# First attention of a two-layer model: the softmax weights are turned undivided and held stationary, the result is divided token by token and turned back

## The reference, cut to what matters

```
logits = einsum('..qhe,..khe->..hqk', q, k) * Dh ** -0.5 + bias      # masked: causal
p = softmax(logits)                                                    # over the keys
out = einsum('..hqk,..khe->..qhe', p, v)
mix = concatenate([y_a, y_b, y_c]); x = x + mix @ w_out
```

## Time and profile before

| | us |
|---|---|
| median of 3 runs | 1622.53 (1620.39 to 1623.35) |
| profiled execution, its own time | 1622.39 |
| its span, first to last instruction | 1620.6 |
| first attention, 221.85 to 293.08 | 71.23 |

### The profile page before, as it was taken

The page is one execution under the profiler, slowest core; times in us unless marked ns, Lnnn a source line. Parts: engine busy times, 40 slices in busy tenths (PEclk is TensorE's granted clock), DMA queues, the critical chain, the costliest instruction groups (busy, mean ns, idle before and its releaser), DMA issues.

```text
span 1620.6 us, 21424 instructions
## 1 busy us (share of the span) xinstructions
PE 1518.1 (94%) x6882; PEld 1184.9 (73%) x6882; DVE 924.2 (57%) x1300; ACT 575.8 (36%) x917; POOL 724.9 (45%) x366
## 2 busy tenths in 40 slices
PE   6989967999999999999988989999899999999997
PEld 4755634777888888888766778666787888888886
DVE  5299977468264554785568351666446655664121
ACT  3322256233231322342476332655223323232222
POOL 1589844434544444434323434535243444444442
PEclk7999979999999999989999999999999999999998
DMA  5588920135455554533323324311132333332332
GB/s 188 145 187 196 224 65 27 52 116 166 151 161 164 162 164 154 169 98 89 82 73 84 81 65 106 53 34 40 52 91 65 104 92 103 91 104 86 96 94 88
DMA packets 285060, 176.72 MB, mean 109 GB/s; under 512 B 43794, under 2 KB 269458, under 8 KB 282954
## 3 DMA queue, kind: packets, MB, share of 16 engines
q1 hardware_dynamic: 285002, 175.98, 39.1%
HBM read 173.29 MB, written 5.80 MB: 111 GB/s over the span
## 4 chain that ended last, share of the span: by engine, by line
PE 40%; issue 36%; POOL 13%; DVE 4%; DMA 3%; ACT 2%; SPq 1%; POOLq 0%; DVEq 0%; ACTq 0%
POOL WL L638 11%; PE ps L1823 11%; PE ps L1825 11%; PE ps L1824 11%; DMA vb<-bv_dram 2%; PE ps L2204 2%; POOL kvp L666 1%; PE ps L2044 1%; PE ps L2018 1%; PE ps L2215 1%; PE ps L2228 1%; DVE qs L1356 1%; DVE scanned L1348 1%; ACT LP L888 1%; DVE LP L1410 1%
## 5 line engine op out<-in xcount | busy, mean ns | idle before, releaser
L638 POOL TENSOR_TENSOR WL<-Wraw,WH 128x1024 fp32r<-128x1024 f32 (+2 forms) x239 | 572.6, 2397 | 797.9 <-ACT WH L760 797.9
L1823 PE MATMUL ps<-actH,WH 128*128 128x512 f32 x1256 | 502.9, 400 | 36.0 <-POOL WL L638 17.1
L760 ACT ACTIVATE WH<-Wraw 128x1024 fp32r<-128x1024 f32 (+2 forms) x239 | 246.1, 1031 | 728.7 <-PE ps L1825 635.5
L1825 PE MATMUL ps<-actH,WL 128*128 128x512 f32 x1256 | 491.6, 391 | 0.0
L1824 PE MATMUL ps<-actL,WH 128*128 128x512 f32 x1256 | 491.4, 391 | 0.0
L1823 PEld LDWEIGHTS ps<-actH,WH 128*128 128x128 f32 x1256 | 237.2, 189 | 116.8 <-issue 25.1
L1825 PEld LDWEIGHTS ps<-actH,WL 128*128 128x128 f32 x1256 | 237.2, 189 | 51.1
L1824 PEld LDWEIGHTS ps<-actL,WH 128*128 128x128 f32 x1256 | 237.6, 189 | 48.5 <-issue 1.9
L1823 PE MATMUL ps<-UH,WH 128*128 128x512 f32 x576 | 228.4, 397 | 10.2 <-DVE T L1677 4.1
L1825 PE MATMUL ps<-UH,WL 128*128 128x512 f32 x576 | 225.7, 392 | 0.0
L1824 PE MATMUL ps<-UL,WH 128*128 128x512 f32 x576 | 225.5, 391 | 0.0
(11 more groups left out here) (236 smaller groups left out, 1531.3 us busy)
## 6 DMA issues: line engine op xcount, KB each, us to landing
Wraw<-in_w_ff SPq DMA_DIRECT2D x64, 512.0 KB, 4.0
Wraw<-in_w_in SPq DMA_DIRECT2D x56, 512.0 KB, 4.0
wada<-in_w_ada SPq DMA_DIRECT2D x64, 384.0 KB, 4.1
Wraw<-in_w_up SPq DMA_DIRECT2D x44, 512.0 KB, 3.8
vb<-bv_dram SPq DMA_DIRECT2D x64, 256.0 KB, 4.5
Wraw<-in_w_down SPq DMA_DIRECT2D x16, 448.0 KB, 3.8
Wraw<-in_w_proj_rnn SPq DMA_DIRECT2D x16, 320.0 KB, 3.1
Wraw<-in_w_proj_mla SPq DMA_DIRECT2D x8, 512.0 KB, 3.9
```

Source lines behind the costliest of these rows:

```text
L638: nc.gpsimd.tensor_tensor(WL[slot][:, 0:kts, :], Wraw[slot][:, 0:kts, :], WH[slot][:, 0:kts, :].bitcast(F32), ALU.subtract).then_inc(s_lo, 1)
L760: A(WH[slot][:, 0:kts, :], Wraw[slot][:, 0:kts, :], ACT.Copy).then_inc(s_hi, 1)
L1823: MM(o, wh, ah, start=first, stop=False)
L1825: return MM(o, wl, ah, start=False, stop=last)
```

## The change

Nobody divides the weights in `LP` any more: `a_normalize` is gone and `a_recips` is one reciprocal a pair (128x8). `a_turn` waits for the exponentials only. `a_weigh` swaps the operands: a turned 128x128 tile of `PT` is stationary, 64 columns of `Vt` move, so bank 7 holds one query a partition and the features of both heads of each block side by side: 20 matmuls in place of 8. The new `a_scaled` on VectorE multiplies bank 7 by the reciprocals, each over 64 columns, into `a_tokens` (the first half of `oSq`, free since the gated attention). The new `a_back` on TensorE turns its four tiles back into bank 7. `pair_high` waits for that. In step p, `a_scaled(p-2)` stands on VectorE where `pair_low(p-2)` stood, `a_back(p-2)` behind the scores of block 3 on TensorE, and `pair_high(p-2)` and `pair_low(p-2)` move to the end of the step: `pair_high` in front of ScalarE's last turned copy, `pair_low` behind VectorE's.

```diff
@@ scalar
-                act.wait_ge(S(pre + "_weighted"), p + 1)
+                act.wait_ge(S("a_turned_back" if pre == "a" else "m_weighted"), p + 1)
@@
-                    if p >= 2 and i == 1:
-                        pair_high("a", p - 2, actH)
                     if 1 <= i and 1 <= p:
                         a_turned(p - 1, i - 1)
+                if p >= 2:
+                    pair_high("a", p - 2, actH)
                 if p >= 1:
                     a_turned(p - 1, TB - 1)
@@ vector
+            def a_recips(p):
+
+                dve.wait_ge(S("a_exp"), 2 * TB * (p + 1))
+                V.reciprocal(astat[:, 2, p % 2, :, :], astat[:, 1, p % 2, :, :]).then_inc(S("a_recip"), 1)
+
+            def a_scaled(p):
+
+                dve.wait_ge(S("a_recip"), p + 1)
+                dve.wait_ge(S("a_weighted"), p + 1)
+                by_head = lambda t: t.rearrange("p (g d) -> p g d", d=HEAD_DIM)
+                V.tensor_tensor(by_head(a_tokens), by_head(ps[:, 7, :]),
+                                astat[:, 2, p % 2, :, :].rearrange("p i e -> p (i e)").unsqueeze(2)
+                                .to_broadcast([P, 2 * TB, HEAD_DIM]), ALU.mult).then_inc(S("a_scaled"), 1)
@@
+                if p >= 2:
+                    pair_low("a", p - 2, actL, actH)
@@ tensor
-                    pe.wait_ge(S(f"a_normed{e}"), TB * p + i + 1)
+                    pe.wait_ge(S("a_exp"), 2 * TB * p + 2 * i + e + 1)
@@
-                for k in range(TB):
+                for i in range(TB):
                     for e in range(2):
-                        q = slice(HEAD_DIM * e, HEAD_DIM * (e + 1))
-                        mm = MM(ps[q, 7, k * P:SEQ], Vt[:, p, k, q], PT[:, e, k, k * P:SEQ], start=(k == 0), stop=(k == TB - 1))
+                        for k in range(i + 1):
+                            mm = MM(ps[:, 7, i * P + e * HEAD_DIM:i * P + (e + 1) * HEAD_DIM], PT[:, e, k, i * P:(i + 1) * P],
+                                    Vt[:, p, k, e * HEAD_DIM:(e + 1) * HEAD_DIM], start=(k == 0), stop=(k == i))
                 mm.then_inc(S("a_weighted"), 1)
+
+            def a_back(p):
+
+                pe.wait_ge(S("a_scaled"), p + 1)
+                for t in range(TB):
+                    mm = nc.tensor.transpose(ps[:, 7, t * P:(t + 1) * P], a_tokens[:, t * P:(t + 1) * P], ident)
+                mm.then_inc(S("a_turned_back"), 1)
...
```

More of the change, by code:

```diff
@@ L345, in hybrid_stack @@
         s_ev = S("block_evacuated")
+        a_tokens = oSq[:, 0:2, :].rearrange("p t c -> p (t c)")
         def wcols(name, rows0, kts):
@@ L677, in _ @@
             lows(gOut, 2, 1)
[L679 to L688, removed]
             pool.wait_ge(S("a_low"), PAIRS)
@@ L1437, in a_step @@
                         a_logits(p, i, 1)
+                    if p >= 1 and i == 0:
+                        a_recips(p - 1)
                     if p >= 2 and i == 2:
[L1439 to L1446, removed]
+                        a_scaled(p - 2)
+                    if p >= 1 and i >= 1:
+                        a_turned(p - 1, i - 1)
                 if p >= 1:
                     a_turned(p - 1, TB - 1)
+                if p >= 2:
+                    pair_low("a", p - 2, actL, actH)
             for p in range(PAIRS + 1):
                 a_step(p)
+            a_scaled(PAIRS - 1)
             pair_low("a", PAIRS - 1, actL, actH)
@@ L2053, in a_step @@
                         a_weigh(p - 2)
+                    if i == 3 and p >= 2:
+                        a_back(p - 2)
                     if i >= 1 and p >= 1:
@@ L2062, in _ @@
             a_weigh(PAIRS - 1)
+            a_back(PAIRS - 1)
             pair_product(gOut, gOut.n0, x_in, lambda k: (S("a_low"), k + 1) if k < PAIRS else (S("gla_low"), k + 1 - PAIRS),
```

## The result

The changed kernel takes 1650.85 us (median of 4 runs, 1647.64 to 1652.13) against 1622.94 (1620.39 to 1626.63): 1.0173 times as long, 95% interval 1.0157 to 1.0188. The forecast was 1634, range 1629 to 1641. The direction was right, the size 2.4 times too small. The profiled execution took 1649.94 us, its span is 1648.2.

What follows compares the result with a forecast made beforehand. The first attention was taken as a loop of waits through TensorE, VectorE and ScalarE, no engine full. Periods +5.8, two end terms +3.2 each and start -0.5 gave +11.7: 1634.1 us, range 1629 to 1641.

Steps and rivals of the forecast that it cites:

- the clock: First attention: no fall in the sum, since TensorE's new gaps are each shorter than the old 1.84 us.
- The loop: First attention, one period: weighing 4.05, turn 0.37, scores of block 2 to next weighing 7.63, together 12.05 us.
- the pace of the weighing: New weighing on TensorE: 40 load-and-multiply pairs at 0.101 us, load-bound, 4.05 us, 1.75 more than before.
- the low part: VectorE, end of each step: the next weighing waits for it, making the loop's tail 7.63 us, not 7.53.
- the turning back: TensorE, behind the scores of block 3: four transposes, 0.56 us, hidden by ScalarE's exponentials except at the end.
- The four periods: First to fifth weighing: 48.2 us at 12.05 each against 42.40 before, +5.8 us.
- the two end terms: Fifth to sixth weighing and last weighing to projection: +3.2 us each.
- the start: Before the first weighing: waits for VectorE between pair 0 and pair 1 go, -0.5 us.
- Rival 1: Weighing goes by its columns, 2.3 us, no loss: 1625.2 us, or 1622 if the clock also rises sooner; chance 7%.
- The prediction's own sign of being wrong: First attention: a granted clock of 0.50 inside the periods, listed among the signs that would show the forecast wrong.
- Rival 2: The clock falls in the new weighings: 8.0 us each, 4 us more per hit, 1638 to 1642 us; chance 12%.
- rivals 3 and 4: New weighing: loads at the transposes' pace, 0.14, 1643.4 us, chance 8%; loads not overlapped, 1647.6 us, chance 3%.

Runs made afterwards that it cites:

- e2: The changed kernel with 128 moving columns instead of 64 in each product of the weighing, waits unchanged, first head's result overwritten: 1637.14 us, ratio 1.0077.
- e6b: The changed kernel with throwaway products only right before each weighing (three, six before the last two): 1634.97 us, ratio 1.008.
- e1: The changed kernel with throwaway products both before the last turn of each pair and before each weighing: 1635.45 us, ratio 1.0067.
- e4: The kernel before, without divisions, with the new form of weighing but no scaling or turning back: 1639.61 us, ratio 1.0078.
- e8: The kernel before with undivided weights and old weighing, dividing its result per feature through eight small products in TensorE's gap: 1617.3 us, ratio 0.9965.

## Why the prediction was wrong

The step that failed is the clock: the sum had no term for its fall, and the fall cost 11.75 us before the projection and 1.2 behind it.

- **The loop: the mechanism right, the close sum luck.** Loads set the pace of the weighing, the low part is the new last wait, the scaling takes 0.60, and the turning back is hidden except at the end: as predicted. But a load and its product take 0.112 us (4.49 / 40), not the 0.101 I took: +0.44 us a weighing. The four periods are 7.6 us longer and not 5.8, the two end terms 3.4 and 3.7 and not 3.2 each. That is 2.5 us more than forecast, and the start gave 2.2 more back, so the parts sum to +12.0 against +11.7 because two errors cancel.
- **A slip in the sum.** The 42.40 us of the four periods before contain their own fall of the clock (4 x 10.20 would be 40.8). The forecast set periods without one against them and so took 1.6 us for a fall that would not come. Rival 1 used 10.20 instead; on the forecast's footing it is 1623.6 and not 1625.2.
- **The start: mis-sized.** -2.7 us instead of -0.5. With the divisions gone TensorE was busy for 4.00 us from 230 to 234 us, before for 2.71, and the clock rose about four microseconds sooner; the prediction names this only inside rival 1. The size is partly chance: counted from the first score product, the first weighing starts after 17.68 us here, 17.29 in e2 and 18.8 in e6b (less its filler), with the same code up to there, and after 20.29 in the kernel before. The rows from 230 to 238 us, before and after:

```profile
230.00:234.00 4.00, 2.71 (x10) 1.30 (x10) 3.42 (x17) 2.62 (x9) 3.11 (x3) 0.50 0.39 133
234.00:238.00 4.00, 4.00 (x13) 1.42 (x10) 2.42 (x10) 2.50 (x10) 1.86 (x3) 0.50 0.00 0
```

```profile
230.00:234.00 4.00, 4.00 (x15) 1.61 (x13) 2.13 (x9) 2.85 (x12) 0.00 (x0) 0.50 0.45 133
234.00:238.00 4.00, 2.44 (x16) 1.47 (x16) 2.30 (x8) 3.30 (x11) 0.00 (x0) 0.99 0.14 23
```

- **The clock: the step that failed.** The prediction's own sign of being wrong, a granted clock of 0.50 inside the periods, is there. Rival 2 had the right price, 4 us for a weighing at the half level (the fifth took 8.56 us where 8.0 was forecast), but 12%, and its 1638 to 1642 holds one or two hits; there were three. The argument was that "TensorE's gaps in the new period ... are each shorter than the 1.84 us" of the old one. They measured 0.1 before the turning back, 1.21 before the last turn (0.5 forecast) and 0.62 before the weighing. So the premise held in every period, and the clock fell all the same: with a pause of 0.62 us before the second weighing, and 1.47 before the fifth and sixth. The argument looked at the idle time only. The new weighing has 64 columns moving under a load of 0.112 us, where 128 take no longer (e2), so its rows read busy while twice the columns would fit in them. e1 and e2 show that either cure, no idle time or twice the columns, kept the clock; e4 shows the clock staying low through a weighing without a pause. How the clock decides is not shown by this.
- **Rival 1** (the weighing goes by its columns) is excluded by the 4.49 us and by e2, rivals 3 and 4 by the 4.49 us. The Trainium skill, "TensorE: Matmul & The Clock Gate", section "Part 3: Packing small matmuls", says that weight loads overlap running matmuls only in other row groups. The traces do not agree: all 40 products here use every row, and 64 more columns in each (e2) made the 40 longer by 0.05 us, where 2560 columns one after another took 2.3 us in the old weighing. So the columns pass while weights are loaded.
- Not settled: why the falls come at the second, fifth and sixth weighing and not at others, which idle time counts, and the 2.6 us lost later in the kernel.

## What to carry to other kernels

Before turning a few wide products into many narrow ones, count the weight loads: 128x128 fp32 loads came at one in 0.112 us, whether 64 or 128 columns moved behind each. In this kernel the clock also fell, or stayed low, in such stretches: price them at both levels, above all where TensorE stands idle just before. When an elementwise step is worth removing, look for a way to do it that keeps the dense product (e8), and put the extra small products where TensorE would have waited.

## What the runs showed that was not expected

Throwaway products that take 1.8 us of TensorE a period made the kernel 15 us faster (1635.45 against 1650.85). A weighing 8.52 us long without a pause stayed at the 1.2 GHz level to its end (e4), where in the kernel before the clock had come back 2.3 us into the old one. And the products of e8, put where TensorE had waited, brought the division back without a loss that the times can tell.
